# Delta rule's five levels on one core: products of 32 columns in place of 64, two X buffers zeroed by POOL, evictions of 256 columns

## The reference, cut to what matters

```python
kk = jnp.einsum('bhnck,bhnsk->bhncs', k, k)
M = jnp.where(strict, beta[..., :, None] * kk * decay, 0.0)
eye = jnp.eye(CHUNK, dtype=jnp.float32)
T = lax.linalg.triangular_solve(eye + M, jnp.broadcast_to(eye, M.shape),
                                left_side=True, lower=True, unit_diagonal=True)
u0 = jnp.einsum('bhncs,bhnsv->bhncv', T, beta[..., None] * v)
wk = jnp.einsum('bhncs,bhnsk->bhnck', T, (beta * jnp.exp(G))[..., None] * k)
...
def step(state, inp):
    u0_c, w_c, qk_c, qd_c, kd_c, gl_c = inp
    u = u0_c - jnp.einsum('bhck,bhkv->bhcv', w_c, state)
    o = jnp.einsum('bhck,bhkv->bhcv', qd_c, state) + jnp.einsum('bhcs,bhsv->bhcv', qk_c, u)
    state = state * gl_c[..., None, None] + jnp.einsum('bhck,bhcv->bhkv', kd_c, u)
    return state, o
```

## Time and profile before

| | us |
|---|---|
| three timed runs | 3860.75, 3865.30, 3864.13 |
| their median | 3864.13 |
| the profiled execution's own time | 3866.55 |
| its span, first to last instruction | 3864.8 |
| PE busy | 3649.1 (94%) |
| DVE busy | 2185.6 (57%) |
| PE's share of the chain that ended last | 83% |
| PE blocks of the levels (line 1784), both layers | 1792 records |

### The profile page before, as it was taken

How to read it: one execution, slowest core, us unless ns; L and a number is a source line. 1 busy time by engine, 2 the same in 40 slices (tenths; PEclk the granted TensorE clock), 3 DMA queues, 4 the chain that set the end, 5 groups by cost and what they waited for, 6 DMA issues and landing times.

```text
span 3864.8 us, 52174 instructions
## 1 busy us (share of the span) xinstructions
PE 3649.1 (94%) x19222; PEld 2939.6 (76%) x19222; DVE 2185.6 (57%) x3533; ACT 1212.9 (31%) x1789; POOL 353.1 (9%) x535
## 2 busy tenths in 40 slices
PE   8988899998988889998999999999999999999999
PEld 6767678886767668886888776788878887667887
DVE  5866578735866578835553566555343336654332
ACT  3342433323342433323222344222222223442221
POOL 1100011100100011100110101111000001010000
PEclk9999999999999999999999999999999999999999
DMA  4300145532300135533553320455333332112333
GB/s 111 79 23 13 39 111 166 151 111 65 85 25 13 38 109 157 159 110 109 166 154 113 88 55 27 117 165 159 108 90 98 89 107 69 44 41 80 98 92 93
DMA packets 580059, 359.84 MB, mean 93 GB/s; under 512 B 20414, under 2 KB 559792, under 8 KB 579888
## 3 DMA queue, kind: packets, MB, share of 16 engines
q1 hardware_dynamic: 554480, 281.43, 26.6%
q0 software_dynamic: 25408, 76.11, 6.6%
HBM read 355.35 MB, written 2.10 MB: 92 GB/s over the span
## 4 chain that ended last, share of the span: by engine, by line
PE 83%; DVE 9%; ACT 3%; issue 2%; DMA 1%; DVEq 1%; ACTq 0%; POOL 0%; SPq 0%; POOLq 0%
PE ps L1351 18%; PE ps L1352 17%; PE ps L1353 17%; PE ps L1600 6%; PE ps L1603 6%; PE ps L1604 6%; PE ps L1784 1%; PE ps L1516 1%; DVE wl L2152 1%; DMA wada<-in_w_ada 1%; PE ps L1496 1%; PE ps L1474 1%; PE ps L1449 1%; PE ps L1563 1%; PE ps L1555 1%
## 5 line engine op out<-in xcount | busy, mean ns | idle before, releaser
L1351 PE MATMUL ps<-hh,wh 128*128 128x512 f32 x3168 | 1260.8, 398 | 49.1 <-DVE wl L2152 22.6
L1353 PE MATMUL ps<-hh,wl 128*128 128x512 f32 x3168 | 1242.5, 392 | 0.0
L1352 PE MATMUL ps<-hl,wh 128*128 128x512 f32 x2912 | 1142.7, 392 | 0.0
L2152 DVE TENSOR_TENSOR wl<-wring,wh 128x1024 fp32r<-128x1024 f32 x500 | 611.4, 1223 | 779.7 <-ACT wh L807 771.9
L807 ACT ACTIVATE wh<-wring 128x1024 fp32r<-128x1024 f32 x528 | 556.6, 1055 | 1031.4 <-PE ps L1353 524.0
L1351 PEld LDWEIGHTS ps<-hh,wh 128*128 128x128 f32 x3168 | 600.4, 190 | 200.8 <-issue 48.2
L1353 PEld LDWEIGHTS ps<-hh,wl 128*128 128x128 f32 x3168 | 600.2, 189 | 128.0
L1352 PEld LDWEIGHTS ps<-hl,wh 128*128 128x128 f32 x2912 | 553.3, 190 | 112.5 <-issue 1.9
L1600 PE MATMUL ps<-ah,wh 128*128 128x512 f32 x1056 | 411.9, 390 | 2.0 <-DVE wl L2152 2.0
L1604 PE MATMUL ps<-ah,wl 128*128 128x512 f32 x1056 | 410.9, 389 | 0.0
L1603 PE MATMUL ps<-al,wh 128*128 128x512 f32 x1056 | 410.9, 389 | 0.0
(11 more groups left out here) (423 smaller groups left out, 3483.8 us busy)
## 6 DMA issues: line engine op xcount, KB each, us to landing
wring<-in_w_ffn_up SPq DMA_DIRECT2D x176, 512.0 KB, 4.9
wada<-in_w_ada POOLq DMA_DIRECT2D x384, 192.0 KB, 2.7
wring<-in_w_in SPq DMA_DIRECT2D x98, 512.0 KB, 5.2
wring<-in_ffn_w_up SPq DMA_DIRECT2D x88, 512.0 KB, 5.0
wring<-in_w_ffn_down SPq DMA_DIRECT2D x64, 512.0 KB, 3.9
wring<-in_w_out SPq DMA_DIRECT2D x32, 512.0 KB, 5.0
wring<-in_ffn_w_down SPq DMA_DIRECT2D x32, 512.0 KB, 3.9
wring<-in_w_ffn_down SPq DMA_DIRECT2D x16, 384.0 KB, 3.4
```

Of the source, the lines that this page charges most:

```text
L1351: pe.matmul(dst, w, h, start=first, stop=False)
L1352: pe.matmul(dst, w, hlo, start=False, stop=False)
L1353: return pe.matmul(dst, wlo, h, start=False, stop=last)
L2152: v.tensor_tensor(wl[:, w, :, :], wring[:, p, h, :, :], wh[:, w, :, :].bitcast(F32), ALU.subtract)\
```

## The change

Of the 64 columns of each product of a level only half can be other than zero or can change: X only in the first L columns of each block of 2L, the same with YT, and Y only in the second L. The changed kernel streams only these 32 columns (`half_of`), packed one after the other in PSUM, so each block fills 256 columns of its bank in place of 512. The weights x stay whole, 64 columns. DVE evicts 256 columns with one operation and writes them back into the half that they belong to. Since an eviction of X now fills only half of `Xm`, the other half must be zero: POOL sets two buffers to zero ahead of the levels, and each again after its use, and DVE's first X eviction of a level also waits for `x_zero`. The second buffer lies where `kb` is written after the levels.

```diff
-        mt, Tm, Xm = halved(kd, 0), halved(kd, 1), halved(kb, 0)
+        mt, Tm = halved(kd, 0), halved(kd, 1)
+        Xm = [halved(kb, 0), halved(kb, 1)]
+
+        def half_of(x, L, o):
+            return x.rearrange("p (b o c) -> p b o c", o=2, c=L)[:, :, o, :]
...
+                    if n == POOL_SPLITS - 2:
+                        g.wait_ge(dn_v.sem, 2)
+                        for i in range(2):
+                            g.memset(Xm[i][:, :, :, :], 0.0).then_inc(x_zero.sem, 1)
+                        for i in range(1, 4):
+                            g.wait_ge(dn_v.sem, dn_count("YT", i, 1))
+                            g.memset(Xm[i % 2][:, :, :, :], 0.0).then_inc(x_zero.sem, 1)
...
-                        m = pe.matmul(ps[r, b, at_], x[r, h, n, :], y[r, h, n, :], start=True, stop=True)
+                        dst = ps[r, b, at_.start // 2:at_.stop // 2].rearrange("p (b c) -> p b c", c=L)
+                        m = pe.matmul(dst, x[r, h, n, :], half_of(y[r, h, n, :], L, o), start=True, stop=True)
...
-                        blocks(ring("X", i, p), p, mt, Tm)
+                        blocks(ring("X", i, p), p, mt, Tm, L, 0)
...
-                        blocks(ring("Y", i, p), p, Xm, Rm)
+                        blocks(ring("Y", i, p), p, X, Rm, L, 1)
                         if i < 5:
-                            blocks(ring("YT", i, p), p, Rm, Xm)
+                            blocks(ring("YT", i, p), p, Rm, X, L, 0)
...
+                    v.wait_ge(x_zero.sem, i if i > 1 else 2)
+                    mask = half_of(cmask[:, i + 2, :], L, 0)[:, None, :, :]
                     for p in range(2):
-                        v.tensor_tensor(pair(Xm, p), made_pair("X", i, p),
-                                        cmask[:, i + 2:i + 3, :].broadcast_to([P, 2 * NT, C]), ALU.mult)\
+                        v.tensor_tensor(pair(Xm[i % 2], p).rearrange("p m (b o c) -> p m b o c", o=2, c=L)[:, :, :, 0, :],
+                                        made("X", i, p)[:, 0:NT * C].rearrange("p (m b c) -> p m b c", m=2 * NT, c=L),
+                                        mask.broadcast_to([P, 2 * NT, C // (2 * L), L]), ALU.mult)\
                             .then_inc(dn_v.sem, 1)
...
-                        v.tensor_tensor(pair(Rm, p), pair(Rm, p), src, ALU.subtract).then_inc(dn_v.sem, 1)
+                        dst = half_pair(Rm, p, 1)
+                        v.tensor_tensor(dst, dst, src, ALU.subtract).then_inc(dn_v.sem, 1)
                         if i < 5:
-                            v.tensor_tensor(pair(Tm, p), pair(Tm, p), made_pair("YT", i, p), ALU.subtract)\
-                                .then_inc(dn_v.sem, 1)
+                            dst = half_pair(Tm, p, 0)
+                            v.tensor_tensor(dst, dst, half_made("YT", i, p), ALU.subtract).then_inc(dn_v.sem, 1)
```

More of the change, by code:

```diff
@@ L433, in program @@
         dn_r = ev("dn_r")
+        x_zero = ev("x_zero")
         rc_ws = ev("rc_ws")
@@ L498, in program @@
                      at_norm, at_turn, at_copied, at_pv, at_out, g_in, g_abs, g_soft, g_cum, g_turn, g_cols,
-                     g_ecol, dn_q, dn_p, dn_v, dn_exp, dn_r, rc_ws, rc_u, rc_o, rc_ds, rc_s, rc_oc, hg_ke,
+                     g_ecol, dn_q, dn_p, dn_v, dn_exp, dn_r, x_zero, rc_ws, rc_u, rc_o, rc_ds, rc_s, rc_oc, hg_ke,
                      hg_eb, hg_qd, o_set, o_hi, o_lo, hg_b, hg_sub, hg_exp, hg_qk, hg_gram, hg_pred, hg_dec, hg_edec,
@@ L1779, in chunks, with blocks @@
                         yield slice(C * e, C * e + C), 2 * p + h, n, slice((NT * h + n) * C, (NT * h + n + 1) * C)
-                def blocks(b, p, x, y):
+                def blocks(b, p, x, y, L, o):
                     for r, h, n, at_ in chunks(p):
-                        m = pe.matmul(ps[r, b, at_], x[r, h, n, :], y[r, h, n, :], start=True, stop=True)
+                        dst = ps[r, b, at_.start // 2:at_.stop // 2].rearrange("p (b c) -> p b c", c=L)
+                        m = pe.matmul(dst, x[r, h, n, :], half_of(y[r, h, n, :], L, o), start=True, stop=True)
                     m.then_inc(dn_p.sem, 1)
@@ L1816, in _ @@
                 for i in range(1, 6):
+                    X, L = Xm[i % 2], LEVELS[i]
                     for p in range(2):
                         have("RT", p) if i == 1 else have("YT", i - 1, p)
-                        blocks(ring("X", i, p), p, mt, Tm)
+                        blocks(ring("X", i, p), p, mt, Tm, L, 0)
                     for p in range(2):
                         have("X", i, p)
-                        blocks(ring("Y", i, p), p, Xm, Rm)
+                        blocks(ring("Y", i, p), p, X, Rm, L, 1)
                         if i < 5:
-                            blocks(ring("YT", i, p), p, Rm, Xm)
+                            blocks(ring("YT", i, p), p, Rm, X, L, 0)
                 for h in range(5):
@@ L2662, in _, with half_pair, half_made @@
                 for i in range(1, 6):
+                    L = LEVELS[i]
+                    def half_pair(x, p, o):
+                        return half_of(pair(x, p).rearrange("p m c -> p (m c)"), L, o)
+                    def half_made(*key):
+                        return made(*key)[:, 0:NT * C].rearrange("p (x c) -> p x c", c=L)
+                    v.wait_ge(x_zero.sem, i if i > 1 else 2)
+                    mask = half_of(cmask[:, i + 2, :], L, 0)[:, None, :, :]
                     for p in range(2):
-                        v.tensor_tensor(pair(Xm, p), made_pair("X", i, p),
-                                        cmask[:, i + 2:i + 3, :].broadcast_to([P, 2 * NT, C]), ALU.mult)\
+                        v.tensor_tensor(pair(Xm[i % 2], p).rearrange("p m (b o c) -> p m b o c", o=2, c=L)[:, :, :, 0, :],
+                                        made("X", i, p)[:, 0:NT * C].rearrange("p (m b c) -> p m b c", m=2 * NT, c=L),
+                                        mask.broadcast_to([P, 2 * NT, C // (2 * L), L]), ALU.mult)\
                             .then_inc(dn_v.sem, 1)
                     for p in range(2):
-                        src = made_pair("Y", i, p)
+                        src = half_made("Y", i, p)
                         if i < 5:
                             made("YT", i, p)
-                        v.tensor_tensor(pair(Rm, p), pair(Rm, p), src, ALU.subtract).then_inc(dn_v.sem, 1)
+                        dst = half_pair(Rm, p, 1)
+                        v.tensor_tensor(dst, dst, src, ALU.subtract).then_inc(dn_v.sem, 1)
                         if i < 5:
-                            v.tensor_tensor(pair(Tm, p), pair(Tm, p), made_pair("YT", i, p), ALU.subtract)\
-                                .then_inc(dn_v.sem, 1)
+                            dst = half_pair(Tm, p, 0)
+                            v.tensor_tensor(dst, dst, half_made("YT", i, p), ALU.subtract).then_inc(dn_v.sem, 1)
                 for h in range(5):
```

## The result

| | before | changed |
|---|---|---|
| timed runs, us | 3860.75, 3865.30, 3864.13, 3862.93 | 3899.20, 3914.02, 3899.59, 3912.48 |
| median | 3863.53 | 3906.03 |
| profiled execution | 3866.55 | 3899.20 |
| its span | 3864.8 | 3897.5 |

The ratio is 1.0111, with a 95% interval of 1.0085 to 1.0138: the change makes the kernel 1.1% slower. The profiled executions differ by 32.65 us. The timed runs of the changed kernel lie in two groups, near 3899 and near 3913, and its profiled execution is of the lower one.

A forecast was written before the change was run, and what follows sets the result against it. PE (83% of the chain) was taken as the bound, its blocks at 1.70 us throughout the levels. 16.0 + 16.7 + 2 = +34.7 us on 3866.55 gives 3901.3, less 2.4: forecast 3899, 8-in-10 range 3868 to 3908.

The forecast's parts named there:

- Streams of 32 columns gain nothing in a block: PE in the levels: the wider of weights and streams sets the time, so a block stays 0.935 us at full clock.
- the third rival: PE in the levels: streams do bind, a block takes 0.47 us, 16 us a layer saved, 3832 us; chance 0.07.
- The clock doesn't come back: PE enters the levels at clock 0.50 and half-empty streams never raise it, so all blocks take 1.70 us.
- The first rival: The levels' clock returns after some 5 us as today, leaving only DVE's gain, 2 x 2.4 us: 3859; chance 0.11.
- the second, one layer only: One layer, or a part of the levels, stays at the low clock; one layer gives 3879; chance of a part 0.14.
- Levels +16.0 and +16.7: 28 blocks at 1.70 us make 47.6 us of levels a layer, against 31.6 in layer 1 and 30.9 in layer 2.
- Behind the levels +1 a layer: Work after the levels starts at low clock; 1 us a layer put on the path, between 0 and 2.9.
- The sum: Both layers' levels and the stretches behind: 16.0 + 16.7 + 2 = +34.7 us on the profiled execution.
- DVE's evictions: Evictions in the levels: 0.42 us for 0.68, 2.4 us a layer at full clock, hidden altogether at low clock.
- the ring: One level's cycle of five PE blocks, then two DVE evictions; 6.33 us before, 5.81 with shorter evictions at full clock.
- POOL at nothing: Five memsets a layer of 0.95 us and DVE's waits on `x_zero` fit into idle time and cost 0.
- From the profiled execution to the median: Last step for the whole kernel: the timed median was put 2.4 us below the profiled execution, 3901.3 to 3899.

The follow-up runs named there:

- e7: The changed kernel plus unused PE matmuls ahead of the levels, four between the RT transposes and one in the 0.64 us pause; 3864.97 us against 3874.33 before.
- e10: The changed kernel with PE streaming 64 columns again and unused matmuls in the pauses ahead of levels and recurrence; 3855.82 us against 3875.85 before.
- e5: The changed kernel again, unaltered, in many runs beside the kernel before on one chip; 3911.86 us against 3874.33, ratio 1.01.
- e1: The changed kernel with PE streaming all 64 columns again, DVE's short evictions and POOL's memsets kept; 3869.51 us against 3871.52 before.
- e2: The changed kernel plus four unused matmuls in PE's 3.65 us pause between the two blocks of transposes; 3868.67 us against 3871.52 before.
- e4: The changed kernel with 64 columns streamed in the first of five levels, 32 in the other four; 3873.14 us against 3871.52 before.
- e8: The kernel of e7 plus six unused matmuls of 512 columns in PE's 5.7 us pause ahead of the recurrence; 3855.55 us against 3874.33 before.
- e11: The same kernel as e8, run again on another chip beside e9 and e10; 3852.47 us against 3875.85 before, ratio 0.9948.
- e9: The kernel before plus unused matmuls in PE's pauses ahead of levels and recurrence (four, one, six); 3858.06 us against 3875.85 before.
- e6: The kernel before plus only POOL's five memsets a layer, each followed by a drain, and DVE's waits on `x_zero`; 3872.30 us against 3874.33.
- e3: The kernel before plus four unused matmuls in PE's pause between the two blocks of transposes; 3871.53 us against 3871.52, ratio 1.0001.

## Why the prediction was right, point by point

The forecast, 3899 with all levels of both layers at 0.50, had the mechanism right, and its main terms fit to 0.4 us. The last step, from there to the median, missed by 9 us (below).

- **Streams of 32 columns gain nothing in a block.** Right. At 0.50 a block was 1.71 us (1.70 forecast), at 1.00 it was 0.935 with 32 columns (e7) and 0.93 with 64 (e10), and the third rival, with its 0.47, falls. That it is the weights which bind is argued from the earlier trace rows and not shown: weight loads are busy 26.39 of 26.80 us in e7's levels of layer 2, but no run narrowed the weights, and a cost of some 29 ns a record whatever its width (0.935 / 32) would look the same in 64 and 32 columns.
- **The clock doesn't come back.** Right: 47.9 of 47.93 us at 0.50 in both layers, twice (changed and e5). e1 shows the cause, not only the coincidence: with 64 columns streamed and all else kept, it came back after 4.3 us. The first rival falls, and so does the second, one layer only: that form came in e2 alone. PE was busy 47.90 of 47.90 us in layer 2's levels and had a clock of 0.50 to the end, so here an engine that always had an instruction was not enough. The price of the lower clock was right too: a block took 1.71 us for 0.935, 1.83 times as long, for a forecast of 1.70. The median record of its weight loads was 223 ns for 135 in e7, 1.65 times, where the forecast said twice.
- **The wording of that step was too wide.** I wrote that half-empty streams "fell or stayed low". They stay low; that they fall is not the rule. e2's layer 1, e4 and e7 hold 1.00 for 21 to 27 us with them. It fell once, in e2's layer 2 behind a pause of 0.64 us, and not in e7, e8 and e11, where that was filled; since e2's layer 1 held behind the same pause, the cause of that fall stays open. The trace of before spoke against the wording too: its recurrence, from whose last 2 us I took it, had been at 1.00 from 335.7 to 364.6 with PE busy 27.89 of 28.90 us. That the array waited for weights half of the time over 363 to 365 was my estimate from 64 columns streamed against 128 of weights; the trace shows only that PE was busy 1.92 and the weight loads 1.78 of these 2.00 us.
- **Levels +16.0 and +16.7.** Measured 47.93 - 31.58 = +16.35 and 47.93 - 30.88 = +17.05, since 28 blocks at 1.71 are 47.9 for my 47.6.
- **Behind the levels +1 a layer.** Right in sum: from the first transpose of the keys to the recurrence it is 350.47 - 328.91 = 21.56 us in layer 1 for 20.06, and 1238.99 - 1218.33 = 20.66 in layer 2 for 20.06, so +1.50 and +0.60. The recurrence itself is +0.14 and -0.34.
- **The sum.** These are 16.35 + 17.05 + 1.50 + 0.60 + 0.14 - 0.34 = 35.3 us, 34.7 forecast, 32.65 measured. Most of the rest lies between the two layers' delta rules: layer 1's recurrence ends about 18.8 us late (0.8 of it from a later start of the levels, 280.98 for 280.15), and layer 2's levels begin only 1170.40 - 1154.72 = 15.68 us late. Most of the 3 us come back in one place, the attention ahead of layer 2's delta rule, where both kernels run the same instructions: in before the clock was 0.50 over 1094 to 1100, in the changed kernel 0.50 over 1110 to 1112 and 0.91 over 1112 to 1114, and from there on 1.00. Across it the changed kernel's lag falls from 17.9 to 15.2 us. The forecast left 2 us for such turns.
- **DVE's evictions.** Right: 0.42 us for 0.68, and hidden at 0.50. Where the clock was full the gain of 2.4 us a layer showed as 2.4 and 2.7 (e9 against e11), and the ring was 5.78 us for a forecast of 5.81 (e7).
- **POOL at nothing.** Right: e6's ratio is 0.9995, and in the changed kernel its memsets are 0.95 us, idle before and after, with no engine waiting for them.
- **From the profiled execution to the median.** This step was wrong by 9.2 us: I took the median 2.4 below the profiled run, but it lies 6.8 above it, since half of the runs are some 13 us longer. The sum was 2.1 too high, which leaves the 7 us between 3899 and 3906. That the median lies within the range owes something to luck: two of the four runs, 3912.48 and 3914.02, are above it, and nothing in the forecast foresaw them. The experiments show one mechanism of nearly that size, 7 to 10 us where it strikes a layer fully: the recurrence, which no edit but e8 to e11 touches, has either some 4 us at 0.50 and takes 33, or 12 to 27 us at 0.50 and takes 37 to 43. Five kernels had this in a profile (e1, e3, e4, e6, e7). The longer runs of the changed kernel themselves weren't profiled, so that they are of this kind is inferred and not shown. Measured against before on its own chip, e5 is 37.5 us longer, nearer to the 34.7 of the sum.

The same recurrence can account for e1, e3 and e4 standing at the time of before though their levels are 3 to 6 us shorter in sum: in these profiles it took 7 to 11 us back. How often it did so in the timed runs, theirs and before's, isn't known. With its entrance filled the gains appear. The kernel with the change and all fills is the fastest that ran, at 0.9957 and 0.9948 of before on two chips, with intervals that end at 0.9971 and below. Of the change it needs DVE's half alone: e10, with full streams on PE, is as fast within the intervals.

## What to carry to other kernels

Before narrowing what a matmul streams, ask whether its streams set its time. Here the weights were as wide as the stream and stayed so: the narrower stream saved no time (0.935 us a block with 32 columns, 0.93 with 64), and where the stage was entered at a granted clock of 0.50 the clock stayed there for as long as the stage lasted, 47.9 us. So read the granted clock at the entrance of each stage with narrow streams, and not only its busy share, which was 100% here. Where such a stage sits behind a pause, a few wide matmuls without use in the pauses (4, 1 and 6 a layer here, in before: 17.8 us by the medians) were worth more than the edit inside the stage (5.6 us on top); the first four alone (e3) brought nothing that showed.

## What the runs showed that I had not expected

- The lower clock is a matter of where one comes from. The same 28 blocks take 26.97 us or 47.93, with the clock at 1.00 or 0.50 at their start. But a start at 1.00 was not enough each time: e2's two layers, alike in their instructions, took 27.26 and 45.58 behind the same pause of 0.64 us.
- A chain of products with 64 or 128 columns against weights of 64 or 128, the recurrence, has both courses in kernels that are alike in it: at 0.50 for its first 3 to 5 us, or for 12 to 27 us, with PE busy 18.78 of 18.80 (e1). What decides between them stays open; with a filled entrance it was at 1.00 in both layers of all four runs (e8 to e11).
- Fills cost nothing visible where they were put: from the first transposes RT of layer 1 to its levels it is 280.62 - 274.04 = 6.58 us in e8, and 280.98 - 274.39 = 6.59 in the changed kernel.
